# Last feed-forward layer by seven half products per pair of weight tiles

## The reference

```python
def swiglu(h, w_in, w_out):
    gate, up = jnp.split(h @ w_in, 2, axis=-1)
    return (jax.nn.silu(gate) * up) @ w_out
...
        h = modulate(rmsnorm(x, norm_ffn_g[i]), sh2, sc2)
        x = x + g2[:, None, :] * swiglu(h, w_ffn_in[i], w_ffn_out[i])
    shf, scf = jnp.split(c_act @ w_ada_final + b_ada_final, 2, axis=-1)
    return modulate(rmsnorm(x, final_norm_g), shf, scf)
```

## Time and profile before

| | |
|---|---|
| median of 3 runs | 1658.89 us (1658.58 to 1659.35) |
| profiled execution, span | 1656.0 us |
| the last FFN in it | 1281.44 to 1642.95 |
| TensorE busy in the span | 1628.9 us, 98% |
| VectorE, ScalarE, GpSimd busy | 804.0, 578.8, 734.7 us |
| granted TensorE clock, mean | 0.996 |

### The profile page before, as it was taken

One profiled execution on the slowest core, in us unless ns is written; L12 is line 12 of the kernel. 1 busy time (PEld: TensorE's weight loads), 2 busy tenths in 40 slices (PEclk: granted clock), 3 DMA queues, 4 the chain that ended last, 5 costly groups with the idle time before them and its releaser, 6 DMA issues.

```text
span 1656.0 us, 21027 instructions
## 1 busy us (share of the span) xinstructions
PE 1628.9 (98%) x7254; PEld 1324.1 (80%) x7254; DVE 804.0 (49%) x1262; ACT 578.8 (35%) x790; POOL 734.7 (44%) x348
## 2 busy tenths in 40 slices
PE   8999999999999999999999999999999999999998
PEld 6785777878888888888888888888888888888886
DVE  6899887878565343433365161451725311111114
ACT  6434434344443322312244233232333431222233
POOL 5999133443244444444444334333424444444442
PEclk9999999999999999999999999999999999999999
DMA  9351266375455565555443223222213232222221
GB/s 383 119 208 65 90 239 212 115 263 206 179 204 190 203 253 192 199 195 187 159 148 107 69 89 101 67 85 78 98 52 96 82 101 94 96 99 92 95 74 61
DMA packets 65442, 233.71 MB, mean 141 GB/s; under 512 B 7264, under 2 KB 7264, under 8 KB 65120
## 3 DMA queue, kind: packets, MB, share of 16 engines
q1 hardware_dynamic: 65376, 232.82, 40.4%
HBM read 230.69 MB, written 2.10 MB: 141 GB/s over the span
## 4 chain that ended last, share of the span: by engine, by line
issue 55%; POOL 30%; PE 8%; DVE 3%; DMA 1%; ACT 1%; POOLq 1%; DVEq 0%; ACTq 0%
POOL w_lo L484 25%; POOL cv_acc L532 2%; PE bank L1542 2%; PE bank L1543 2%; PE bank L1544 2%; DVE mods_ring L1066 1%; POOL cv_y L514 1%; POOL diag L526 1%; POOL sq L526 1%; DVE x L1108 0%; DMA w_raw<-pl_v_in 0%; ACT sq L585 0%; DMA mods_ring<-w_mods_in 0%; PE bank L1573 0%; PE bank L1577 0%
## 5 line engine op out<-in xcount | busy, mean ns | idle before, releaser
L484 POOL TENSOR_TENSOR w_lo<-w_raw,w_hi 128x1024 fp32r<-128x1024 f32 x268 | 644.7, 2411 | 875.3 <-ACT w_hi L576 864.6
L1542 PE MATMUL bank<-h_hi,w_hi 128*128 128x512 f32 x1240 | 485.4, 391 | 1.2 <-POOL h_lo L496 0.9
L1544 PE MATMUL bank<-h_hi,w_lo 128*128 128x512 f32 x1240 | 482.7, 389 | 0.0
L1543 PE MATMUL bank<-h_lo,w_hi 128*128 128x512 f32 x1240 | 482.6, 389 | 0.0
L576 ACT ACTIVATE w_hi<-w_raw 128x1024 fp32r<-128x1024 f32 x264 | 277.8, 1052 | 261.1 <-PE bank L1544 242.8
L1542 PEld LDWEIGHTS bank<-h_hi,w_hi 128*128 128x128 f32 x1240 | 232.8, 188 | 51.7 <-issue 2.5
L1543 PEld LDWEIGHTS bank<-h_lo,w_hi 128*128 128x128 f32 x1240 | 232.8, 188 | 49.3 <-issue 1.2
L1544 PEld LDWEIGHTS bank<-h_hi,w_lo 128*128 128x128 f32 x1240 | 232.8, 188 | 48.5
L1542 PE MATMUL bank<-f_hi,w_hi 128*128 128x512 f32 x472 | 184.7, 391 | 0.9 <-DVE z_buf L1448 0.9
L1543 PE MATMUL bank<-f_lo,w_hi 128*128 128x512 f32 x472 | 185.0, 392 | 0.0
L1544 PE MATMUL bank<-f_hi,w_lo 128*128 128x512 f32 x472 | 183.6, 389 | 0.0
(11 more groups left out here) (271 smaller groups left out, 1847.6 us busy)
## 6 DMA issues: line engine op xcount, KB each, us to landing
mods_ring<-w_mods_in SPq DMA_DIRECT2D x152, 512.0 KB, 6.2
w_raw<-ff_in_in SPq DMA_DIRECT2D x88, 512.0 KB, 3.5
w_raw<-ret_in SPq DMA_DIRECT2D x64, 512.0 KB, 3.5
w_raw<-ff_out_in SPq DMA_DIRECT2D x32, 512.0 KB, 3.5
w_raw<-cv_ab_in SPq DMA_DIRECT2D x16, 512.0 KB, 6.3
w_raw<-ff_tail_in SPq DMA_DIRECT2D x16, 384.0 KB, 3.0
w_raw<-cv_g_in SPq DMA_DIRECT2D x8, 512.0 KB, 3.5
w_raw<-cv_out_in SPq DMA_DIRECT2D x8, 512.0 KB, 3.4
```

The source lines that it names most:

```text
L484: pool.tensor_tensor(w_lo[:, s, :], w_raw[:, s, :], w_hi[:, s, :].bitcast(F32), ALU.subtract).then_inc(lo_done, 1)
L1542: pe.matmul(out, w_h, m_h, start=start, stop=False)
L1543: pe.matmul(out, w_h, m_l, start=False, stop=False)
L1544: return pe.matmul(out, w_l, m_h, start=False, stop=stop)
```

## The change

All of the last FFN but its first four tiles is computed on pairs of tiles. A pair holds two weight tiles, whose blocks are taken as 2 x 2: even and odd input chunks (columns of the two by two weights), first and second tile (rows). The right side is 2 x 2 too: even and odd chunk of h or z, first and second half of the 512 tokens. With A the weights and B the right side,

- S1 = A21 + A22, S2 = S1 - A11, S3 = A11 - A21, S4 = A12 - S2
- T1 = B12 - B11, T2 = B22 - T1, T3 = B22 - B12, T4 = B21 - T2
- seven products A11 B11, A12 B21, S1 T1, S2 T2, S3 T3, A22 T4, S4 B22, each over half the blocks (512 weight columns, 384 in the last part) and 256 tokens: 12 (9) matmuls of 256 columns.

S2 T2 is summed onto bank 0 behind A11 B11, after ScalarE copied that bank out (p1); A22 T4 onto bank 2 behind S3 T3, S4 B22 onto bank 3 behind S1 T1 (copied as p5). VectorE makes t7 = bank 2 + p5, c11 = bank 1 + p1, c22 = bank 0 + t7, c21 = bank 2 + u2, c12 = bank 3 + u2, where u2 is ScalarE's copy of bank 0. In an in pair, c21 and c22 are the gate halves and c11 and c12 the up halves of one chunk; z goes to `sq` (even chunks) and `ssum` (odd). In an out pair each c is added to a half of one x chunk.

p1, p5, u2, t7 and the c lie in SBUF, in halves of h tiles that are no longer needed; the weight sums lie in `rb`, `diag`, `dg_rest` and in place in `w_raw`, all SBUF; the token sums of z in `c_all`, which is PSUM. Of each pair ScalarE rounds seven half blocks and GpSimd makes seven rests of 128 x 512 (384). The weight sums of the first two pairs are made by GpSimd, of the others by VectorE. The norm ahead writes all eight chunks to `h_raw`, from which VectorE, ScalarE and VectorE again make the token sums `ht_hi`, `ht_lo`. The weights' layout in memory is changed to even chunks first; bytes and loads stay. There are 20 in pairs (gate and up tile of one chunk each), 8 out pairs of 512 and 4 of 384. The code is unrolled.

```diff
+PAIRS = [x for p, n in enumerate(PARTS)
+         for x in ([("in", p, c) for c in range(0 if p else 2, n)] + [("out", p, m) for m in range(0, DC, 2)])]
+half_width = lambda q: PARTS[PAIRS[q][1]] // 2 * P if PAIRS[q][0] == "out" else 4 * P
...
+        s1_of = lambda q: w_raw[:, 2 * (q % 2) + 1, 0:half_width(q)]
+        s2_sum, s3_sum, s4_sum = rb, diag, dg_rest[:].rearrange("p q n -> p (q n)")
+        z_pair = (sq, ssum)
+        t_sums = c_all
+        def left_raw(q, j):
+            h, even, odd = half_width(q), 2 * (q % 2), 2 * (q % 2) + 1
+            return (w_raw[:, even, 0:h], s3_sum[:, 0:h], s1_of(q), w_raw[:, even, h:2 * h], s2_sum[:, 0:h],
+                    w_raw[:, odd, h:2 * h], s4_sum[:, 0:h])[j]
+        def left_block(w, q, j):
+            return w[:, j // 2, (j % 2) * T:(j % 2) * T + half_width(q)]
...
+            def half_lo_parts(q):
+                for j in range(BLOCKS):
+                    pool.wait_ge(s_hi, BLOCKS * q + j + 1)
+                    pool.tensor_tensor(left_block(w_lo, q, j), left_raw(q, j), left_block(w_hi, q, j).bitcast(F32),
+                                       ALU.subtract).then_inc(s_lo, 1)
...
+            def half_hi(q, j):
+                if q >= len(PAIRS):
+                    return
+                if j in (LEFT_A11, LEFT_A12, LEFT_A22):
+                    act.wait_ge(raw_in[2 * (q % 2) + (j == LEFT_A22)], 16 * (N_UNITS // SLOTS + q // 2 + 1))
+                else:
+                    act.wait_ge(s_sum, 4 * q + 1 + (LEFT_S3, LEFT_S1, LEFT_S2, LEFT_S4).index(j))
+                if q:
+                    act.wait_ge(half_done, BLOCKS * (q - 1) + j + 1)
+                else:
+                    wait_unit(act, "in10", j // 2)
+                act.activation(left_block(w_hi, q, j), left_raw(q, j), ACT.Copy).then_inc(s_hi, 1)
+            def copy_half(q, j, b, to, read_by):
+                act.wait_ge(half_done, BLOCKS * q + j + 1)
+                if q:
+                    act.wait_ge(combined, 5 * (q - 1) + read_by)
+                act.activation(to, bank[b][:, 0:H], ACT.Copy).then_inc(copied, 1)
...
+                for q, (kind, p, n) in enumerate(PAIRS):
+                    c = sum(PARTS[:p]) + n - 1 if kind == "in" else sum(PARTS[:p + 1]) - 1 if n == 0 else None
+                    if c is not None and kind == "out":
+                        chunk_hi(c)
+                        sums_hi(c)
+                    copy_half(q, LEFT_A11, 0, p1, 2)
+                    half_hi(q + 1, 0)
+                    if kind == "in" and c is not None and (n or p == 0):
+                        chunk_hi(c)
+                    half_hi(q + 1, 1)
+                    if c is not None and kind == "in" and n and n % 2 == 0:
+                        sums_hi(c)
+                    copy_half(q, LEFT_S1, 3, p5, 1)
+                    half_hi(q + 1, 2)
+                    half_hi(q + 1, 3)
+                    copy_half(q, LEFT_S2, 0, u2, 5)
+                    half_hi(q + 1, 4)
+                    if kind == "in":
+                        act.wait_ge(combined, 5 * q + 3)
+                        act.activation(c22, c22, ACT.Silu).then_inc(gated, 1)
+                        act.wait_ge(combined, 5 * q + 4)
+                        act.activation(c21, c21, ACT.Silu).then_inc(gated, 1)
+                    half_hi(q + 1, 5)
+                    half_hi(q + 1, 6)
...
+            def left_sums(q, which):
+                if q < 2 or q >= len(PAIRS):
+                    return
+                a11, a12, a22 = left_raw(q, LEFT_A11), left_raw(q, LEFT_A12), left_raw(q, LEFT_A22)
+                s1, h, n = s1_of(q), half_width(q), 4 * q
+                before = BLOCKS * (q - 1)
+                if which == 0:
+                    for s in (2 * (q % 2), 2 * (q % 2) + 1):
+                        v.wait_ge(raw_in[s], 16 * (N_UNITS // SLOTS + q // 2 + 1))
+                    v.wait_ge(s_lo, before + LEFT_S3 + 1)
+                    v.tensor_tensor(s3_sum[:, 0:h], a11, s1, ALU.subtract).then_inc(s_sum, 1)
+                    v.wait_ge(s_sum, n + 1)
+                    v.tensor_tensor(s1, s1, a22, ALU.add).then_inc(s_sum, 1)
+                else:
+                    v.wait_ge(s_sum, n + 2)
+                    v.wait_ge(s_lo, before + LEFT_S2 + 1)
+                    v.tensor_tensor(s2_sum[:, 0:h], s1, a11, ALU.subtract).then_inc(s_sum, 1)
+                    v.wait_ge(s_sum, n + 3)
+                    v.wait_ge(s_lo, before + LEFT_S4 + 1)
+                    v.tensor_tensor(s4_sum[:, 0:h], a12, s2_sum[:, 0:h], ALU.subtract).then_inc(s_sum, 1)
+            def chunk_lo(c):
+                k = c % 8
+                cols = slice(0, T) if c % 2 else FRONT
+                v.wait_ge(ft_hi_done, 3 * (c // 2) + c % 2 + 1)
+                v.tensor_tensor(f_lo[:, k, cols], z_pair[c % 2][:, cols], f_hi[:, k, cols].bitcast(F32),
+                                ALU.subtract).then_inc(ft_lo_done, 1)
+            def chunk_sums(c):
+                n = 2 * (c - 1)
+                b11, b12, b21, b22 = (z[:, cols] for z in z_pair for cols in (FRONT, BACK))
+                t1, t3, t4, t2 = (t_sums[:, i * H:(i + 1) * H] for i in range(4))
+                v.wait_ge(z_made, c + 1)
+                if c > 1:
+                    v.wait_ge(ft_lo_done, 3 * (c // 2))
+                v.tensor_tensor(t1, b12, b11, ALU.subtract).then_inc(t_sum, 1)
+                v.tensor_tensor(t3, b22, b12, ALU.subtract).then_inc(t_sum, 1)
+                v.wait_ge(t_sum, n + 1)
+                v.tensor_tensor(t2, b22, t1, ALU.subtract).then_inc(t_sum, 1)
+                v.wait_ge(t_sum, n + 3)
+                v.tensor_tensor(t4, b21, t2, ALU.subtract).then_inc(t_sum, 1)
+            def sums_lo(c):
+                k = (c - 1) % 8
+                rows = lambda b: b[:, k:k + 2, :].rearrange("p a n -> p (a n)")
+                v.wait_ge(ft_hi_done, 3 * (c // 2 + 1))
+                v.tensor_tensor(rows(ft_lo), t_sums[:], rows(ft_hi).bitcast(F32), ALU.subtract).then_inc(ft_lo_done, 1)
...
+                for q, (kind, p, n) in enumerate(PAIRS):
+                    half = lambda j: v.wait_ge(half_done, BLOCKS * q + j + 1)
+                    done = lambda i: v.wait_ge(combined, 5 * q + i)
+                    half(LEFT_S1)
+                    v.wait_ge(copied, 3 * q + 2)
+                    if q:
+                        v.wait_ge(combined, 5 * (q - 1) + 3)
+                    v.tensor_tensor(t7, bank[2][:, 0:H], p5, ALU.add).then_inc(combined, 1)
+                    def update(c, cols, value):
+                        v.scalar_tensor_tensor(x[:, c, cols], value, gate(n5, c), x[:, c, cols], ALU.mult,
+                                               ALU.add).then_inc(x_part, 1)
+                    half(LEFT_A12)
+                    if q and PAIRS[q - 1][0] == "in":
+                        v.wait_ge(z_made, sum(PARTS[:PAIRS[q - 1][1]]) + PAIRS[q - 1][2] + 1)
+                    elif q:
+                        v.wait_ge(x_part, 4 * sum(k == "out" for k, _, _ in PAIRS[:q]))
+                    v.tensor_tensor(c11, bank[1][:, 0:H], p1, ALU.add).then_inc(combined, 1)
+                    if kind == "out":
+                        done(2)
+                        update(n, FRONT, c11)
+                    half(LEFT_S2)
+                    v.wait_ge(copied, 3 * q + 3)
+                    done(1)
+                    v.tensor_tensor(c22, bank[0][:, 0:H], t7, ALU.add).then_inc(combined, 1)
+                    if kind == "out":
+                        done(3)
+                        update(n + 1, BACK, c22)
+                    half(LEFT_A22)
+                    v.tensor_tensor(c21, bank[2][:, 0:H], u2, ALU.add).then_inc(combined, 1)
+                    if kind == "out":
+                        done(4)
+                        update(n + 1, FRONT, c21)
+                    early = kind == "in" and n < PARTS[p] - 1 or kind == "out" and n < DC - 2
+                    if early:
+                        left_sums(q + 2, 0)
+                    half(LEFT_S4)
+                    v.tensor_tensor(c12, bank[3][:, 0:H], u2, ALU.add).then_inc(combined, 1)
+                    done(5)
+                    if kind == "in":
+                        c = sum(PARTS[:p]) + n
+                        z = z_pair[c % 2]
+                        if c % 2 == 0:
+                            v.wait_ge(ft_lo_done, 3 * (c // 2))
+                        v.wait_ge(gated, 2 * (sum(k == "in" for k, _, _ in PAIRS[:q])) + 2)
+                        v.tensor_tensor(z[:, FRONT], c11, c21, ALU.mult)
+                        v.tensor_tensor(z[:, BACK], c12, c22, ALU.mult).then_inc(z_made, 1)
+                        if c % 2:
+                            chunk_lo(c - 1)
+                            chunk_sums(c)
+                            chunk_lo(c)
+                            sums_lo(c)
+                    else:
+                        update(n, BACK, c12)
+                        if p == len(PARTS) - 1:
```

(47 more changed lines are left out.)

217 lines of the change are left out of this document (194 added, 23 removed).

## The result

Before 1659.12 us (1658.58 to 1659.88), changed 1742.76 us (1742.31 to 1743.39), four runs each on one chip: the ratio is 1.0507, 95% interval 1.0492 to 1.0522. The forecast was 1722 with a range of 1662 to 1765, so the middle is missed by 21 us. Between the same two matmuls as in the earlier trace rows the stage of the last FFN runs from 1282.49 to 1724.51 in the profiled execution: 442.0 us in place of 361.5 (+80.5). The whole span is 84.9 us longer; 1.1 of the rest lie ahead of the stage and 3.3 behind it, in the final norm.

What follows compares the result with a forecast made beforehand. TensorE, busy 98%, was taken to bound the kernel until VectorE and GpSimd hold each other up. Stage: 21.9 + 4 + 10 x 26.5 + 8 x 12.1 + 35.8 + 1 = 424.5 against 361.5, +63: 1722 us, range 1662-1765.

Steps and rivals of the forecast that it cites:

- TensorE's price: Last FFN's matmuls: 2604 of 256 columns at 0.118 us replace 1488 at 0.2282, -32.5 us if TensorE stays the bound.
- the faster rival: TensorE stays the bound as waiting VectorE operations slip into GpSimd's gaps: period 9.9, -25, 1633 us; chance 0.13.
- The turns: VectorE operations with two SBUF inputs and GpSimd's rests exclude each other; a 512-wide turn pair costs 1.70 us.
- The walk of two in pairs: VectorE's queue followed from t7 to t7: even pair 10.0 us, odd 16.5, together 26.5 against 21.9; chance 0.45.
- rival 1: The port alone bounds, VectorE never late: GpSimd with turns 11.3 us per in pair, +18, 1677 us; chance 0.20.
- rival 2: TensorE's clock falls to half behind the odd pair's 6 us gap: 3 us ten times, +30, 1752 us; chance 0.18.
- Out pairs: Eight out pairs of 512: four updates and four sums each take a turn, 12.1 us a pair against 10.95.
- Last four and the end: Pairs of 384 estimated at 10.1, 10.1, 8.0 and 7.6 us against 8.2 each; the end 0.4, in the rounding.
- The start: Token sums of h under the first tiles meet GpSimd's first rests; t7, wanted at 1310.4, comes 4 us late.

Runs made afterwards that it cites:

- e1_one_input: Against the changed kernel, VectorE's weight sums of all pairs but the last four read one operand from PSUM, giving other values: 1705.7 us, ratio 1.0261 to 1.0299.

## Why the prediction was right, and where it was off

**TensorE's price: right.** 0.118 us a matmul, 9.8 us a pair when nothing waits. With start and ends in, the faster rival said -25; with short rests and sums it is -22.6.

**The turns: right, and the main cause.** GpSimd's rests with 512 columns took 1.28 us free, 1.42 to 1.49 with a turn of 256 columns and 1.67 to 1.77 with one of 512 (walk: 1.27, 1.42 and 1.70). Shortening GpSimd's rests brings 98 us, more than the whole loss of 84; taking VectorE's weight sums out of the turns, with GpSimd's rests left whole, brings 37.

**The walk of two in pairs: right to 1.4 us, in part by luck.** 26.5 was forecast from t7 to t7. Where the long gaps stand it was 27.4 to 27.9; in the timeline above 10.99 in the even pair (forecast 10.0) and 16.84 in the odd one (16.5). The difference is the clock: behind the gap A22 and what follows run at half clock, and c21 comes 3.5 us behind t7 in the even pair, where the walk had 2.05; with the gaps filled the period is 26.2 to 26.3. In the odd pair two errors nearly cancel: c21 came 3.3 us behind t7 and not 2.05, and from there to the next t7 it took 13.5 us where the walk has 14.45. The ten periods together are 268.3 us where 265 was forecast: the regular ones are longer and those at a part's start or end shorter (24.2 to 26.8, except for the very first, 29.2).

**What the walk said of the cause in its queue was half right.** It had t7 queued behind S4, and against rival 1 "t7 behind s4 in its queue". Moving t7 ahead brought nothing: another bank's release is late then. What counts is VectorE's whole chain in the odd pair, and moving work off that chain to where VectorE waits for A22 brought 24 us.

**The clock (rival 2): it fell, but cost less.** Priced at 3 us for each of ten gaps, measured 1.2 to 1.4 in seven. The stretch is shorter (3.4 us at 0.50, then 2.7 at 0.76: 2.3 us of work lost), and the rest of the difference must lie under VectorE's chain; that part is argued. The rival's 1752 was too far by 9, the walk's 1722 too low by 21: the range holds because both were in it. That the main sum had no term for the clock left out about 9 us in the seven gaps that were filled. Behind the gaps at the heads of the out parts the clock fell too (0.50 to 0.56 over 3.4 us), and in the final norm; what that cost was not measured. The earlier trace rows showed the fall, and it should have been in the sum.

**Out pairs: under-sized.** The walk counts from t7 to t7. Counted so, the eight out pairs took 101.4 us where 96.8 + 1 was forecast, 11.4 to 14.9 each (forecast 12.1). An update of x under rests shows mostly 0.7 to 1.1 us, a sum of weights that meets a rest 1.64 to 1.78:

```profile
1429.93 1.07 DVE L1690 SCALAR_TENSOR_TENSOR x<-over_h_lo,mod,x 128x256 f32<-128x256 f32 x1
1430.93 1.78 DVE L1593 TENSOR_TENSOR diag<-w_raw 128x512 f32<-128x512 f32 x1
1432.74 1.65 DVE L1595 TENSOR_TENSOR w_raw<-w_raw 128x512 f32<-128x512 f32 x1
```

**Last four and the end: the largest error in proportion.** The last four periods were forecast as 10.1, 10.1, 8.0 and 7.6. From t7 to t7 the first three took 11.9, 11.0 and 8.6. The walk left out what VectorE does there besides: the squares for the final norm, two for each of the first three pairs with a wait for ScalarE between, ahead of S2, S4 and t7 (VectorE's timeline):

```profile
1707.27 0.69 DVE L1203 TENSOR_TENSOR ps_bc<-ps_bc,sq 128x512 f32<-128x512 f32 x1
1708.71 0.70 DVE L1203 TENSOR_TENSOR ps_bc<-ps_bc,sq 128x512 f32<-128x512 f32 x1 [0.76 <-ACT sq L670]
```

That is 2.1 us a pair (0.69 + 0.76 + 0.70) on VectorE's chain; that it is all of the 3.3 us by which the three are longer was not tested. The end was put at 0.4 us and into the rounding. The last matmul of the products starts at 1722.49 and the first statistics matmul 2.0 us later, behind two updates of x and the last of these sums; before, the two stood 0.2 us apart. The same 2.0 us stand in every run of the new form, also with short rests and sums, so the turns do not make them.

**The start: 7 us where 4 was forecast, and at another product.** TensorE stands still for 6.1 us ahead of S1 T1, which needs bank 3, and that waits for VectorE's z of the second standard chunk (L1653 at 1312.51), not for t7; t7 follows at 1318.45, where it was wanted at 1310.4 plus the 1.1 us by which the stage began later. That z stands behind token sums and rests of `ht_lo` that meet GpSimd's first rests: four sums took 5.24 us where four of the same shape took 1.67 before them, two rests 4.50 where two took 2.44 (VectorE's timeline):

```profile
1301.52 5.24 DVE L1671 SCALAR_TENSOR_TENSOR h_raw<-h_raw,mod 128x256 f32<-128x256 f32 x4
1306.68 4.50 DVE L1647 TENSOR_TENSOR ht_lo<-h_raw,ht_hi 128x1024 fp32r<-128x1024 f32 x2
```

The errors by part, cut at t7 as the walk is: up to the first t7 +3.0 us (36.0 against 21.9 + 4 and the 7.1 from the first pair's start to where t7 was wanted), in pairs +3.3, out pairs +3.6, from the last four's first t7 to the end +7.7 (36.4 against 35.8 less those 7.1). That is 17.5, the distance from 424.5 to 442.0. The 4.4 us ahead of and behind the stage had no term at all.

## What to carry to other kernels

Fewer multiplications are paid for on the engines that prepare the operands. Count, for each period, the two-input SBUF operations of VectorE beside GpSimd's, give each meeting its turn, and then walk VectorE's whole queue once through the longest period, norm and statistics included: busy shares of 64% and 53% of the whole run (85% and 76% in the stage) hid a chain with no slack. If such a chain sets the pace, first try to move work to where that engine waits: here that brought 24 us with nothing made cheaper, and sparing the two products their turns 6.

## What the runs showed of the hardware

A 256-column VectorE product with two SBUF inputs, 0.42 us alone, takes up to 1.55 beside GpSimd's 512-column rests; GpSimd's rest pays 0.2 (256 columns) to 0.5 (512) for each meeting. Of the weight sums with one operand in PSUM (e1_one_input) neither is seen: 0.68 and 0.69 us each, and not one of GpSimd's rests of 1.67 to 1.77 us is left in the in pairs and out pairs of 512. The Trainium skill's rule (SBUF — State Buffer, Who interferes with whom), that the two exclude each other for a whole instruction, agrees with this.

Behind a gap of 5.7 us TensorE had 3.4 us at 0.50 clock and 2.7 us at a mean of 0.76, in net 1.2 to 1.4 us of time here. It was not expected that more and shorter gaps would lift the mean clock: with the spread work and the products in PSUM TensorE still stands still for 55 us of the stage against 80, but the mean granted clock of the run is 0.985 against 0.969.
